# Normalising the next unit ahead of a later unit's maximum on VectorE, in the sparse attention of a two-block transformer

## What is computed

```
s = jnp.einsum('qghd,gkd->ghqk', qf, k_win) * scale + t5_bias(dist, rel_tbl)
p = masked_softmax(s, mask)
o_win = jnp.einsum('ghqk,gkd->qghd', p, v_win)
...
return gt[..., 0:1] * o_cmp + gt[..., 1:2] * o_sel + gt[..., 2:3] * o_win
```

## Time and profile before

| | |
|---|---|
| Median of 3 runs | 2777.19 us (2776.22 to 2777.63) |
| The profiled execution | 2774.93 us |
| Its span | 2773.1 us |
| Mean granted TensorE clock | 0.943 of full |
| TensorE matmuls, VectorE, ScalarE busy over the span | 89%, 63%, 40% |
| First instruction of the units on VectorE | 812.98 us |
| First matmul of the output projection | 899.60 us |

### The profile page before, as it was taken

One profiled execution on the slowest core, in us unless ns is written; L12 is line 12 of the kernel. 1 busy time (PEld: TensorE's weight loads), 2 busy tenths in 40 slices (PEclk: granted clock), 3 DMA queues, 4 the chain that ended last, 5 costly groups with the idle time before them and its releaser, 6 DMA issues. The chain is left out here.

```text
span 2773.1 us, 46189 instructions
## 1 busy us (share of the span) xinstructions
PE 2476.9 (89%) x18921; PEld 2373.5 (86%) x18921; DVE 1751.5 (63%) x2571; ACT 1103.3 (40%) x1550; POOL 74.4 (3%) x127
## 2 busy tenths in 40 slices
PE   7937558999798689997999999999999989999998
PEld 6836457999786589997998888999999988898998
DVE  5546435777546357775776556667777755756776
ACT  4421224333446243334333555443343345555332
POOL 1000000000000000000002100000000030000000
PEclk9968877999999789999999999999999999999999
DMA  8400024555470145552555423455545463235542
GB/s 227 150 0 1 0 64 142 186 182 182 125 177 16 49 152 182 182 182 93 183 181 144 137 90 107 138 182 170 168 160 169 165 168 99 92 108 168 175 162 87
DMA packets 294978, 370.55 MB, mean 134 GB/s; under 512 B 15321, under 2 KB 263634, under 8 KB 294674
## 3 DMA queue, kind: packets, MB, share of 16 engines
q1 hardware_dynamic: 289584, 355.24, 39.2%
q0 software_dynamic: 4880, 13.13, 2.7%
q10 hardware_dynamic: 370, 0.11, 0.0%
HBM read 360.59 MB, written 7.86 MB: 133 GB/s over the span
## 5 line engine op out<-in xcount | busy, mean ns | idle before, releaser
L291 PE MATMUL psum_banks<-source_high,weights_high 128*128 128x272 f32 (+1 forms) x3680 | 1078.2, 293 | 85.1 <-DVE weights_low L476 25.6
L292 PE MATMUL psum_banks<-source_low,weights_high 128*128 128x272 f32 (+1 forms) x3680 | 1066.0, 290 | 0.0
L293 PE MATMUL psum_banks<-source_high,weights_low 128*128 128x272 f32 (+1 forms) x3680 | 1065.6, 290 | 0.1
L291 PEld LDWEIGHTS psum_banks<-source_high,weights_high 128*128 128x128 f32 x3680 | 711.2, 193 | 96.3 <-DVE weights_low L476 26.8
L292 PEld LDWEIGHTS psum_banks<-source_low,weights_high 128*128 128x128 f32 x3680 | 711.7, 193 | 0.2
L293 PEld LDWEIGHTS psum_banks<-source_high,weights_low 128*128 128x128 f32 x3680 | 710.6, 193 | 0.3 <-issue 0.3
L291 PE MATMUL psum_banks<-hidden_high,weights_high 128*128 128x272 f32 (+1 forms) x1216 | 349.8, 288 | 0.2 <-DVE h L1028 0.2
L293 PE MATMUL psum_banks<-hidden_high,weights_low 128*128 128x272 f32 (+1 forms) x1216 | 348.6, 287 | 0.0
L292 PE MATMUL psum_banks<-hidden_low,weights_high 128*128 128x272 f32 (+1 forms) x1216 | 347.4, 286 | 0.0
L1002 DVE TENSOR_TENSOR weights_low<-weight_ring,weights_high 128x2048 fp32r<-128x2048 f32 x131 | 292.9, 2287 | 73.7 <-ACT weights_high L996 73.5
L996 ACT ACTIVATE weights_high<-weight_ring 128x2048 fp32r<-128x2048 f32 x131 | 242.5, 1912 | 196.2 <-PE psum_banks L293 185.5
(11 more groups left out here) (419 smaller groups left out, 2958.5 us busy)
## 6 DMA issues: line engine op xcount, KB each, us to landing
weight_ring<-ffn_w_in SPq DMA_DIRECT2D x88, 1024.0 KB, 6.7
weight_ring<-w_in SPq DMA_DIRECT2D x48, 1024.0 KB, 5.2
weight_ring<-ffn_w_out SPq DMA_DIRECT2D x44, 1024.0 KB, 5.0
weight_ring<-moe_w_gate SPq DMA_DIRECT2D x32, 1024.0 KB, 6.3
weight_ring<-moe_w_up SPq DMA_DIRECT2D x32, 1024.0 KB, 7.4
weight_ring<-moe_w_down SPq DMA_DIRECT2D x32, 1024.0 KB, 5.0
weight_ring<-gdn_w_in SPq DMA_DIRECT2D x16, 1024.0 KB, 6.2
weight_ring<-w_branch SPq DMA_DIRECT2D x12, 1024.0 KB, 5.0
```

The source lines that it names most:

```text
L291: pe.matmul(out, w_hi, x_hi, start=start, stop=False)
L292: pe.matmul(out, w_hi, x_lo, start=False, stop=False)
L293: return pe.matmul(out, w_lo, x_hi, start=False, stop=stop)
```

## The change

VectorE's list for a step is written in another order: `normalise(u + 1)` comes first, then the fill tiles and `out_low(u - 1)` as before, and `max_of(u + 2)` comes last. The other engines' lists and all waits stay as they are.

```diff
                 max_of(1)
                 normalise(0)
                 for u in range(n_units):
-                    if u + 2 < n_units:
-                        max_of(u + 2)
+                    if u + 1 < n_units:
+                        normalise(u + 1)
                     for t in NSA_FILL.get(u, []):
                         take(t)
                     if u:
                         out_low(u - 1)
-                    if u + 1 < n_units:
-                        normalise(u + 1)
+                    if u + 2 < n_units:
+                        max_of(u + 2)
                 out_low(n_units - 1)
```

## The result

| | before | changed |
|---|---|---|
| Median of 4 runs | 2777.32 us | 2805.96 us (2805.45 to 2808.13) |
| Profiled execution, its span | 2774.93, 2773.1 | 2806.38, 2804.5 |
| Loop: start of the first add to start of the last `out_low` | 86.14 us | 119.07 us |
| From the first add to the end of the last normalising | 78.16 us | 109.04 us |
| Mean granted TensorE clock | 0.943 | 0.939 |

The changed kernel is slower: ratio 1.0105, 95% interval 1.0088 to 1.0123, which is 24 to 34 us; the medians lie 28.6 apart and the two profiled executions 31.5. The loop grew by 32.9 us (812.98 to 899.12 before, 813.76 to 932.83 after), the rest of the span shrank by 1.5.

The account below looks back on a forecast made before the run. No engine was full, VectorE nearest, so the order of hand-overs decides. Open waits of 41.2 less 13.5 gone gave 28 us, plus 5 for TensorE's clock: 33, so 2807.9 profiled and 2810 median; range 2800 to 2821.

Parts of the forecast that it names:

- the open exponentials: VectorE, branch units: each exponential waited for uncovered, 1.80 us short and 2.23 long, eight of each, 32.2 us.
- the lost overlap of 0.09: VectorE: the instruction after a maximum's reduce starts 0.09 us before it ends; lost at a wait.
- The pooled two: Pooled units in mid-loop, with a short exponential: 1.1 us left open; the two at the start nothing.
- The fills: Fill tiles 18 and 20: VectorE waits 0.8 and 0.3 us for a panel's high part, 1.1 together.
- out_low: VectorE waits for out_high at out_low of units 5, 9 and 15: 1.8, 3.0 and 2.0, sum 6.8 us.
- The sum at the full clock: Loop's last normalising: 41.2 us of open waits after, less 13.5 gone, ends 27.7, say 28 us later.
- The clock: TensorE at the lower level for most of the loop: 4.6, say 5 us more; bounds 0 and 9.
- The total: Whole kernel: 28 + 5 = 33 us longer, profiled execution 2807.9, median 2810.2; chance 0.65.
- A: Rival: TensorE's clock stays high where it counts; +28 us, 2805; chance 0.15.
- B: Rival: low clock everywhere, TensorE itself late for turned_out; +37 to 41 us, about 2816; chance 0.13.
- C: Rival: faster, as the turns' 8.8 us of waits for normalising go; 2768; chance 0.03.
- D: Rival: no difference, old out_high waits shield the new or a later weight wait absorbs the shift; 2777; chance 0.04.

Follow-up runs that it names:

- M N F P: Kernel before with each step ordered maximum, normalise, fill tiles, then out_low taken one step later, last in the step; 2778.91 us, ratio 1.0007.

## Why the prediction was right, and where its sizes were off

**The main term, the open exponentials.** Forecast 1.80 and 2.23 us each, with the lost overlap of 0.09: the trace has 1.71 and 2.14 of idle time, the same numbers less the overlap. Sixteen of them were to be 32.2; the row says 31.6, and with sixteen overlaps 33. The 0.7 more is unit 7, whose exponential stood behind a late `turned_out` (2.41 in place of 1.71); this I had left out. The pooled two left 1.3 open, for 1.1.

**The fills.** Forecast 1.1, measured 0.9.

**out_low.** At the full clock 6.8 was forecast. Measured at the real clock: 1.57, 0.30, 2.98, 0.79 and 3.42 at units 5, 7, 9, 13 and 15, together 9.1; with the clock's part in my sum (2.0, 1.0 and 0.6) it was 10.4. All the units named are there, each within 0.6. With TensorE kept busy, near the full clock, those at units 5, 9 and 15 are 1.57, 2.98 and 1.77, where 1.8, 3.0 and 2.0 were forecast.

**The sum at the full clock.** 28 was forecast. The two experiments with TensorE kept busy give this difference almost by itself: 113.48 less 84.56, 28.9 us. It is not quite the full clock: in the busy changed kernel the weighings of units 7 and 13 still ran partly at the low level, and the old order was kept busy only at its end.

**The clock.** Forecast 5, with bounds 0 and 9. The difference of the loops, 32.9, less those 28.9, is 4.0, and rough for the same reason. Inside the loop it was less than thought (keeping busy took 2.0 off up to the last normalising, 109.04 to 107.04, where I had 3.6), at its end more: 3.6, for the last turn and weighing, of which the kernel before also pays 1.5, so 2.1 net. I had counted only the turn, 1.0. The low level came as expected, 0.52 and 0.63 between 880 and 900. But 870 to 880 and 910 to 920 had 1.00, where I had written 0.5 to 0.7 all the way from 855 to 925. The Trainium skill, TensorE: Matmul & The Clock Gate, Part 1, has the low level follow an idle stretch, by which the weighing of unit 15 might have kept the full clock. It did not: it began low at 904.20, right behind scores that took 1.13, the full one. The gap ahead of these scores was 2.38 us, and 0.51 the one before it.

**The total.** Forecast 33 for the loop, measured 32.9. That it is so close is in part luck: the exponentials came out 0.8 above their forecast and the end of the loop 1.1 above, the waits for `out_high` 1.3 below. The profiled execution was to be 2807.9 and was 2806.4. The median was forecast at 2810 and is 2806.0, 28.6 above before. The weak step is the last one, the median taken as the profiled execution plus 2.26: that gap lay within the spread of single executions and did not carry over (the changed kernel's median lies 0.4 below its profiled execution).

**The rivals.** A, the clock stays high: its 2805 is near the median, but the windows and the busy experiments show that the clock fell and cost 4 us in the loop. The time alone could not have told it from the forecast. B, low everywhere: not so, 1.00 in 870 to 880 and 910 to 920. C, faster: the turns' waits did go (8.8 to 5.1), and did not pay, since an open exponential cost 1.7 to 2.1 and not under 0.7. D, taken up later: the output products began 33.7 us later (933.31 against 899.60) and the span grew by 31.4; SP's queue waited for slots even longer, up to 92.5 us in 812 to 955:

```profile
SPq L359 <- DVE weights_low L1832: 143.1, 6, 92.5
```

**Open.** Why the medians moved 28.6 and the loops 32.9 is not settled. The two don't contradict each other, since the interval of the time is 24 to 34 us. But the median less the loop goes from 2686.0 to 2691.6 over the twelve kernels (2691.2 before, 2686.9 changed), and in five of the ten experiments the growth of the loop lies outside the interval of the time, in three of them by 1.5 us or more: M N F P, its copy with transposes, and the old order with transposes at its end. Each loop was profiled once, so it is not known whether the loop differs from one execution to the next or the rest does.

## What to carry to other kernels

Where an engine hands work to another and gets it back (here maximum, exponential, normalising), the list must put something independent between giving and taking; count for each round trip what stands between the two in the list, also across the turn of the loop. An instruction that waits for the slowest chain of the step belongs where little is queued behind it that others need, yet early enough for whoever waits for its buffer: `out_low` one step later and first in the step gained 4 us in the loop, one step later and last lost 6. A wait that a reordering removes is worth something only if the engine that waited was on the path.

## What the runs showed of the hardware that I had not expected

TensorE's granted clock also fell in the midst of unbroken work. In the changed kernel with extra transposes the scores of unit 10 and the weighing of unit 7 behind them ran without a gap from 867.46 on, at the full clock, and from some 869.6 on at the low one:

```profile
869.28 0.27 PE L2048 MATMUL psum_banks<-cmp_probs_turned,cmp_values 128*64 128x128 f32 x1
869.39 0.81 PE L2045 MATMUL psum_banks<-probs_turned,values 128*64 128x256 f32 x3
869.66 1.06 PE L2048 MATMUL psum_banks<-cmp_probs_turned,cmp_values 128*64 128x128 f32 x4
```
```profile
868.00:870.00 2.00, 2.00 (x17) 1.72 (x17) 0.66 (x1) 1.31 (x5) 0.00 (x0) 0.91 0.04 8
870.00:872.00 2.00, 2.00 (x10) 1.24 (x8) 1.13 (x3) 1.15 (x5) 0.00 (x0) 0.50 0.00 0
```

Four matmuls of one kind take 0.60 at the full clock and 1.06 here. The gap ahead of 867.46 had been 2.70 us, and no longer gap stands near: here the fall came some 2 us after the idle time had ended, and it hit the busy piece behind it. The weighing of unit 15 in the changed kernel is a second case, low 1.1 us after a gap of 2.38 us. And code that is the same in every kernel took 2684 to 2692 us outside the loop, so that a change of under some 5 us in this program is better read from its stretch of the profile than from the time.
